# Half of an output projection cut into portions between recurrence levels, and the S5 stages placed one projection unit later

## What is computed

```
proj = rms_norm(h) @ w_in_even                # 1024 -> 512 (S5) + 4 x 512 (q, f, i, g)
y_a = gelu(s5(u)); y_a = y_a * sigmoid(y_a @ w_glu + b_glu)    # S5: diagonal state space
y_b = hgrn2(q, f, i, g)                       # 4 heads of 128, gated linear recurrence
h = h + concat([y_a, y_b]) @ w_out_even       # 1024 -> 1024
```

## Time and profile before

| engine | busy, us | share of the span |
|---|---|---|
| PE | 2472.5 | 95% |
| DVE | 1179.6 | 45% |
| POOL | 851.5 | 33% |
| ACT | 554.0 | 21% |

### The profile page before, as it was taken

The page is one execution under the profiler, slowest core; times in us unless marked ns, Lnnn a source line. Parts: engine busy times, 40 slices in busy tenths (PEclk is TensorE's granted clock), DMA queues, the critical chain, the costliest instruction groups (busy, mean ns, idle before and its releaser), DMA issues.

```text
span 2593.6 us, 32665 instructions
## 1 busy us (share of the span) xinstructions
PE 2472.5 (95%) x13054; PEld 2004.6 (77%) x13054; DVE 1179.6 (45%) x1189; ACT 554.0 (21%) x858; POOL 851.5 (33%) x497
## 2 busy tenths in 40 slices
PE   8999967899999999999997999989999999999997
PEld 6877856688888888888885776668888888888885
DVE  6888179432432422424617355652432332424625
ACT  3110255311001011011212145632001001011215
POOL 3634322132333333333322334552333333333321
PEclk9978978999999999999998999999999999999998
DMA  7362441211111111111112211021111111111211
GB/s 213 89 103 67 108 131 43 98 49 49 49 49 49 49 49 49 49 48 48 59 49 89 49 25 57 17 73 49 49 49 49 46 46 48 47 48 49 65 49 65
DMA packets 249160, 159.65 MB, mean 62 GB/s; under 512 B 32132, under 2 KB 236136, under 8 KB 249064
## 3 DMA queue, kind: packets, MB, share of 16 engines
q1 hardware_dynamic: 236248, 142.31, 19.1%
q10 hardware_dynamic: 12832, 16.19, 2.6%
HBM read 131.81 MB, written 25.49 MB: 61 GB/s over the span
## 4 chain that ended last, share of the span: by engine, by line
PE 86%; DVE 8%; issue 2%; ACT 2%; POOL 1%; DMA 1%; ACTq 1%; POOLq 0%; DVEq 0%; SPq 0%
PE ps L618 69%; PE ps L1097 3%; PE ps L769 2%; PE ps L1129 2%; PE ps L1057 1%; DVE hg_queries_keys L1862 1%; PE ps L1070 1%; PE ps L1081 1%; PE ps L790 1%; PE ps L685 1%; PE ps L742 1%; PE ps L994 1%; DVE stage L1544 1%; DVE s_state L1614 1%; ACT x_hi L1180 1%
## 5 line engine op out<-in xcount | busy, mean ns | idle before, releaser
L481 POOL CAST w_hi<-w_raw 128x1024 fp32r<-128x1024 f32 x198 | 217.8, 1100 | 1466.4 <-PE ps L618 1125.1
L618 PE MATMUL ps<-x_hi,w_hi 128*128 128x512 f32 x1600 | 497.2, 392 | 6.4 <-issue 3.2
L618 PE MATMUL ps<-x_lo,w_hi 128*128 128x512 f32 x1600 | 494.1, 390 | 0.0
L618 PE MATMUL ps<-x_hi,w_lo 128*128 128x512 f32 x1600 | 493.7, 390 | 0.0
L483 POOL TENSOR_TENSOR w_lo<-w_raw,w_hi 128x1024 fp32r<-128x1024 f32 x198 | 486.6, 2458 | 15.9
L618 PE MATMUL ps<-mid_hi,w_hi 128*128 128x512 f32 x1216 | 376.0, 391 | 8.7 <-DVE mid_lo L1914 5.8
L618 PE MATMUL ps<-mid_lo,w_hi 128*128 128x512 f32 x1216 | 375.4, 390 | 0.0
L618 PE MATMUL ps<-mid_hi,w_lo 128*128 128x512 f32 x1216 | 375.4, 390 | 0.0
L618 PEld LDWEIGHTS ps<-x_hi,w_hi 128*128 128x128 f32 x1600 | 300.3, 188 | 73.5 <-issue 8.8
L618 PEld LDWEIGHTS ps<-x_lo,w_hi 128*128 128x128 f32 x1600 | 301.2, 188 | 62.9
L618 PEld LDWEIGHTS ps<-x_hi,w_lo 128*128 128x128 f32 x1600 | 300.9, 188 | 62.9
(11 more groups left out here) (285 smaller groups left out, 2511.1 us busy)
## 6 DMA issues: line engine op xcount, KB each, us to landing
w_raw<-w_mlp_in_in SPq DMA_DIRECT2D x64, 512.0 KB, 4.0
w_raw<-w_mlp_out_in SPq DMA_DIRECT2D x64, 512.0 KB, 3.9
w_raw<-w_in_even_in SPq DMA_DIRECT2D x20, 512.0 KB, 4.5
residual_dram<-residual ACTq DMA_DIRECT2D x2, 4096.0 KB, 13.1
fqig_dram<-stage SPq DMA_DIRECT2D x16, 512.0 KB, 3.1
w_raw<-w_ple_gate_in SPq DMA_DIRECT2D x16, 512.0 KB, 3.9
x_tokens<-x_in SPq DMA_DIRECT2D x8, 512.0 KB, 7.3
w_raw<-w_out_even_in SPq DMA_DIRECT2D x8, 512.0 KB, 4.4
```

Of the source, the lines that this page charges most:

```text
L481: pool.tensor_copy(WH[:, b, :], RAW[:, b, :]).then_inc(S["w_hi_done"], 1)
L618: ins = pe.matmul(acc[:, h, :], w[:, k, :], x[:, k0 + k, h * HALF:(h + 1) * HALF], start=(k == 0 and w is wh and x is xh), stop=(k == kts ...
```

## The change

- PE takes unit 11 before the transposes of the end weights, and each later unit one place earlier: 12 behind the kernel matmuls, 13 between the two end states, 14 and 15 before the outputs, 16 to 19 as half units in the output steps. No unit stands between the last output step and the GLU product.
- Units 15 to 19 are no longer copied by ACT and scaled on POOL: DVE multiplies the accumulator by the scale (`unit_out`). Their writes to DRAM (and that of 15) are issued by ACT.
- The output projection is cut in two. The S5 half (4 of 8 k-tiles, `out_first`) is made in bank 3 alone, in half units of 12 matmuls, two portions of FILL = 6 matmuls each, put behind `level` in two of three slots from the pass of head 1 on. ACT copies each of the 16 results and writes it to `part_dram` (`parts`). Its slabs hold 512 rows x 256 columns, for two units.
- The tail's transposes and squares of both halves now share bank 2, with waits between them.
- At the end SP loads H and the parts in 16 DMAs of 512 KB, POOL adds them tile by tile (`add_out_part`), and PE runs eight units of 24 matmuls for the other half.

```diff
-            for s in range(6, 11):
+            for s in range(6, 12):
                 one(s, s, XA)
@@ PE, kernel matmuls, end states, outputs
-            one(11, 11, XA)
+            one(12, 12, XA)
-                    one(12, 12, XA)
+                    one(13, 13, XA)
-            one(13, 13, XA)
             one(14, 14, XA)
+            one(15, 15, XA)
-                half_unit(15 + n // 2, n % 2)
-            one(19, 19, XA)
+                half_unit(16 + n // 2, n % 2)
@@ PE, tail of a head (key_tokens)
+                pe.wait_ge(S["hg_v_copied"], 2 * hd + 2)
+                if half:
+                    pe.wait_ge(S["hg_k_copied"], u)
@@ PE, value_tokens
+                if half:
+                    pe.wait_ge(S["hg_v_copied"], u)
@@ PE
+            def out_first():
+                pe.wait_ge(S["mid_ready"], 8)
+                for m in range(KT):
...
+                    for h in range(2):
+                        if m + h:
+                            pe.wait_ge(S["opart_copied"], 2 * m + h)
+                        for k in range(4):
+                            for w, x in ((wh, XBh), (wh, XBl), (wl, XBh)):
...
+                                ins = pe.matmul(PS[:, 3, :], w[:, k, :], x[:, k, h * HALF:(h + 1) * HALF],
...
+                        if hd and (2 * LEVELS * (hd - 1) + 2 * l + half) % 3 < 2:
+                            dense(first, FILL)
...
+            for m in range(KT):
+                u = UNIT["out"] + m
...
+                unit(ACC[m % 2], wh, wl, XBh, XBl, kts=4, k0=4)
@@ ACT
-                    head_unit(15 + n // 2)
+                    spill(16 + n // 2)
-            head_unit(19)
+                while copied[0] < 2 * KT and 3 * copied[0] + 1 <= 2 * LEVELS * (hd - 1) + slot:
...
+                    fn(o, PS[:, 3, :], ACT.Copy).then_inc(S["opart_copied"], 1)
+                    act.wait_ge(S["opart_copied"], j + 1)
+                    act.dma_start(part_dram[m * P:(m + 1) * P, h * HALF:(h + 1) * HALF], o).then_inc(spilled[m % 2], 16)
@@ DVE
+            for u in (15, 16, 17):
+                unit_out(u)
             for k in range(3):
                 gelu_in(k)
                 gelu_out(k)
+                if k < 2:
+                    unit_out(18 + k)
@@ POOL
+            for m in range(KT):
+                add_out_part(m)
+                if m in (2, 4):
+                    one(SLAB["out"] + 5 + m // 2, UNIT["out"] + m, "acc_done")
@@ SP
-            sp.dma_start(H[:, :, :], h_dram.rearrange("(k p) t -> p k t", p=P)).then_inc(S["h_restored"], 16)
+            for m in range(KT):
+                sp.dma_start(H[:, m, :], h_dram[m * P:(m + 1) * P, :]).then_inc(tile_loaded[m], 16)
+                sp.dma_start(OPART[:, m, :], part_dram[m * P:(m + 1) * P, :]).then_inc(tile_loaded[m], 16)
+            out_half(1, 2)
+            out_half(1, 3)
```

More of the change, by code:

```diff
@@ L41 @@
 LAG = 2
+FILL = 6
 V_STEP = 12
@@ L540, in _, with add_out_part @@
                 gate_mult(hd)
[L541 to L546, removed]
+                if hd == 0:
+                    one(SLAB["out"], 22)
+                    one(SLAB["out"] + 1, 24)
+                if hd:
+                    one(SLAB["out"] + hd + 1, 4 * hd, "opart_done")
+            one(SLAB["out"] + 5, 16, "opart_done")
+            def add_out_part(m):
+                pool.wait_ge(tile_loaded[m], 16 * 3)
+                pool.tensor_tensor(H[:, m, :], H[:, m, :], OPART[:, m, :], ALU.add).then_inc(S["out_part"], 1)
+            for m in range(KT):
+                add_out_part(m)
+                if m in (2, 4):
+                    one(SLAB["out"] + 5 + m // 2, UNIT["out"] + m, "acc_done")
             run(SLAB["mlp0"], UNIT["mlp0"], 64)
@@ L1133, in wo_first @@
                                 yield
-            def dense(work, count):
-                for _ in range(count):
-                    next(work, None)
             pe.wait_ge(S["ss_read"], 4)
@@ L1392, in _ @@
                 value_copy(0, half)
[L1393 to L1418 removed]
+            copied = [0]
@@ new lines, in _ @@
+            for half in range(2):
+                forget(1, half)
+            for half in range(2):
+                direct_copy(0, half)
+            for hd in range(1, HEADS + 1):
+                now, tail = hd < HEADS, hd - 1
+                key_copy(tail, 0)
+                parts(hd, 0)
+                key_copy(tail, 1)
+                parts(hd, 1)
+                if now:
+                    gate(hd)
+                for half in range(2):
+                    parts(hd, 2 + 2 * half)
+                    if hd < HEADS - 1:
+                        forget(hd + 1, half)
+                parts(hd, 6)
+                for half in range(2):
+                    squares(tail, half)
+                    if now:
+                        value_copy(hd, half)
+                    parts(hd, 8 + half)
+                act.preload_act_table_set("natural_log_exp_and_others")
+                for half in range(2):
+                    head_rstd(tail, half)
+                    parts(hd, 10 + half)
+                if now:
+                    direct_copy(hd, 0)
+                    parts(hd, 12)
+                    direct_copy(hd, 1)
+                parts(hd, 13)
+                for half in range(2):
+                    y_high(tail, half)
@@ L1419, in _ @@
+            assert copied[0] == 2 * KT
             finish(1, "mlp", 0)
@@ L2056, in embed @@
                 end_norm()
-            dve.wait_ge(S["h_restored"], 16)
-            residual(UNIT["out"], 1, ("mlp", 0), None)
+            for b in range(2):
+                dve.wait_ge(spilled[b], 16 * (10 + KT))
+            residual(UNIT["out"], 1, ("mlp", 0), None, parts=True)
             mlp("mlp0", 1, 8, (2, ("ple", 0)))
```

132 lines of the change are left out of this document (76 added, 56 removed).

## The result

The changed kernel takes 2603.16 us (median; 2598.84 to 2604.5) against 2590.66 for the kernel before: 1.0043 times as long, 95% interval 1.0031 to 1.0055. Later runs on the same kernels gave 2599.79 against 2589.80, ratio 1.0037 (1.0023 to 1.0051). It is **slower** by 10 to 12.5 us, under half a per cent, but clear of the interval. The forecast was 2587.0, faster by 3.6, with a range up to 2602: the first median lies 1.2 us outside it, the second 2.2 inside, and the sign of the likeliest case was wrong.

The account below looks back on a forecast made before the run. PE was taken as the bound, busy 2472.5 us, leaving only its idle and lower-clock time to win. Terms 4.2 + 4.2 + 24.9 + 2.5 - 39.4 = -3.6 took the median from 2590.56 to 2587.0 us; 8-in-10 range 2574 to 2602.

Parts of the forecast that it names:

- the likeliest case: Whole kernel: faster than before by more than 5.2 us, chance 0.42; the author's own sum, chance 0.40, was -3.6 us.
- S5 stages: From 147 us: transposes -5.9, kernel matmuls -3.5, hole +10.7, GLU half clock +2.6, ACT waits 0.3; sum +4.2 us.
- head 0: Recurrence's first head, no portions: 3.0 us for two DVE updates meeting POOL's splits, 1.2 for ACT's copy; +4.2 us.
- heads 1 to 3: Recurrence with portions of 1.36 us: PE becomes the bound, heads take 32.7, 31.9 and 31.3 us; +24.9 us.
- last tail: End of recurrence: four portions fill idle time, but both halves' copies and roots go serially through bank 2; +2.5 us.
- output projection: Last y_low to the MLP's first unit's end: 100.9 us falls to 61.5 (58 to 66); -39.4 us.
- I don't add both: Output projection: late-slab stall of 3.2 us and DVE-chain excess of 6.5 overlap, so 61.5 us was taken.
- hole: PE idle between the last output step and the GLU, with unit 19 moved into the steps; about 10.7 us.
- rival two's mechanism: S5 kernel matmuls keep full clock to their end, winning 9 us instead of 3.5; 2581 to 2579 us, chance 0.11.
- DVE's chain hangs on the end of the kernel matmuls: S5 stages: DVE starts when the Toeplitz tile lands, so the first output step stays 59.4 us behind the kernel matmuls.
- nearly free filler: Heads 1 to 3 grow by 15 us, not 25, as dense matmuls start over drain; 2577 us, chance 0.22.
- The handshake: Recurrence portions: late ACT copies of bank 3 add about 0.75 us per half unit, 16 times; 2599 us, chance 0.22.

Follow-up runs that it names:

- second pair: The changed kernel and the kernel before, both unaltered, profiled once more; later medians 2599.79 against 2589.80 us, ratio 1.0037.
- s5_only: The kernel before with only the S5 side of the change, old recurrence and output projection; 2593.41 us, 1.0006 times the kernel before.
- s5_gap_behind: The kernel before with only the change's S5 side, plus a PE wait between last end-weight transpose and first kernel matmul; 2609.44 us, one run.
- s5_gap_inside: The kernel before with only the change's S5 side, plus a PE wait between end-weight transposes 16 and 17; 2597.93 us, one run.

## Why the prediction was wrong, point by point

The terms as forecast and as the first profile of after has them; of the first row 1.4 us more lie upstream of it, as unit 10 ends at 148.46 and not at 147.01.

| term | forecast | measured |
|---|---|---|
| S5 stages | +4.2 | -3.9 |
| head 0 | +4.2 | +7.0 |
| heads 1 to 3 | +24.9 | +28.9 |
| last tail | +2.5 | +3.2 |
| output projection | -39.4 | -31.4 |
| rest | 0 | -1.8 (+1.1 in the second pair) |

**The step that failed most is the output projection**, the term that carried the gain. Its bare sum of 57.0 was right: 57.2 without adds and late slab. The stalls on top were taken as 4.5 and are 12.3. I priced DVE's chain by the attention's projection, 6.5 us over its PE time; there three of the eight units' chains were stretched beside POOL; in after it were five, with four splits and eight adds between the first matmul and the MLP, and a wait of 4.68 for an add besides. "I don't add both" was right, but of two bounds the longer counts, and this one I had not measured by the row that I had used for head 0: an operation of DVE waits out POOL's. The slab stall itself was near (3.2 forecast, 4.7 measured in after). What showed in its place: stalls of 12.3 us instead of 4.5, of which the adds alone make 12.6 and the late slab alone 7.2, one over the other.

**The recurrence**, 31.6 forecast and 39.1 measured. Heads 1 to 3 took 33.8, 32.8 and 33.4 for 32.7, 31.9 and 31.3: the mechanism (PE becomes the bound, busy over 90%; it was 93%) held, the term was 4.0 short. I had the waits at 7.5 us in sum and PE was idle for 6.5; what was short is the work, 30.4, 29.0 and 29.0 us forecast for 31.9, 29.5 and 32.0 busy. In head 0 I counted two collisions and 3.0 us; the two splits met four operations, at 5.6 us. The bank's 1.2 there was right (1.3 and 1.4). The last tail was 0.7 short.

**The S5 stages** missed the other way, by 8.1. Transposes 3.83 (4.3 forecast) and hole 10.0 (10.7) held. The kernel matmuls won 9.4 in place of 3.5: rival two's mechanism, at 0.11 the least likely. I had read from the earlier trace rows that narrow work doesn't hold the clock; the earlier trace rows only showed that it doesn't raise it, and in the earlier trace rows PE had idled in between. 2.8 us of it were given back, since the first output step came 62.2 us behind the kernel matmuls' end and not 59.4: the second half of the state matmuls waited 4.9 for DVE. The step that failed there is that DVE's chain hangs on the end of the kernel matmuls: in before it had idled 1.86 us for the Toeplitz tile, in after it began without idle time, held by its own work beside POOL:

```profile
196.80 3.30 DVE L1701 TENSOR_TENSOR s_rotation<-s_rotation,stage 128x1024 f32<-128x1024 f32 x1
200.13 1.23 DVE L1701 TENSOR_TENSOR stage<-ps,s_rotation 128x1024 f32<-128x1024 f32 x1
```

That is 23.9 us behind the kernel matmuls' end, where it was 17.6. The wait at the first output step shrank to 2.7 us, where I had said about 6. The output steps were 2.3 shorter (80.96 for 83.26) and the GLU lost 1.2 by its half clock, not 2.6.

**The rivals.** The nearly free filler was wrong: +28.9, not +15. The kernel matmuls' clock was right, and did not bring its 2579 because of the other two terms. The handshake was wrong: three waits of L941 for ACT's copy, 2.6 us in all in after. The time came out near its 2599, but for another reason. The sum of -3.6 less 8.1, plus 7.5, 8.0 and 1.4 upstream, less 1.8 behind, is the +3.5 of the profiles: two misses on the one side hid behind one on the other. The further 6.5 to 9 us of the medians lie in the spread of both kernels' runs. About 3 us on either side have a stage, the one behind the projection and its granted clock; the others have none.

## What to carry to other kernels

A filler put into a latency-bound stretch pays only for the idle time that it covers. Of 38.1 us of matmuls in heads 1 to 3, 9.2 were covered, and the stage that they left was held up by its elementwise chain at 69.5 where PE alone needs 57. Before moving dense work, ask what its old place was covering: unit 19 covered the GLU's chain, and putting it back was worth 11 to 16 us, about what the whole change cost. A small filler is not a cheap one: a third of the matmuls cost 16.4 of the 28.9 us. Keep POOL's two-operand work away from the stretch in which DVE's chain sets the pace, and put dense work, not a gap, straight ahead of a long stretch of narrow matmuls.

## What the runs showed of the hardware

- The same 64 x 16 matmuls, without a gap, took 13.1 us when entered at granted 1.00 (s5_only, after) and 22.4 when entered at 0.50 (before, s5_gap_behind). They neither raised nor lowered the clock, with the one exception of s5_gap_inside, where it rose 0.1 us after they began.
- DVE beside POOL: operations of 0.68 and 1.22 us with two operands in SBUF took 2.84 and 3.41, while a residual that reads PSUM kept 1.23. The Trainium skill has this in "SBUF — State Buffer", section "SBUF: two separate sides": the pair of ports that the two share is an exclusive lock held for the whole instruction. The traces agree. What they add is the sum: 5.6 us in head 0, 12.6 in the projection by the adds.
- A transfer that was thought to bind need not: loading the slabs ahead took away a wait of 4.7 us and moved the stage by 0.3, as long as DVE's chain beside the adds was the longer. Without the adds the same edit won 7.2.
